# Gated DeltaNet and Hyena layer on one core: in levels two to five of the triangular inverse, VectorE's 32x32 block transposes in place of a ScalarE copy and TensorE transposes

## The reference

```python
kk = jnp.einsum('nbhid,nbhjd->nbhij', kc, kc)
a_strict = jnp.where(strict, bc[..., :, None] * kk * jnp.exp(diff), 0.0)
lower_unit = a_strict + jnp.eye(GDN_CHUNK, dtype=a_strict.dtype)
rhs = jnp.concatenate([vc * bc[..., None], kc * (bc * jnp.exp(gcum))[..., None]], axis=-1)
sol = lax.linalg.triangular_solve(lower_unit, rhs, left_side=True, lower=True, unit_diagonal=True)
```

## Time and profile before

| | us |
|---|---|
| runs | 1676.72, 1670.04, 1681.54; median 1676.72 |
| span of the profiled execution | 1665.2 |
| of it the heads and the tail | 162.8 to 775 |

### The profile page before, as it was taken

How to read it: one execution, slowest core, us unless ns; L and a number is a source line. 1 busy time by engine, 2 the same in 40 slices (tenths; PEclk the granted TensorE clock), 3 DMA queues, 4 the chain that set the end, 5 groups by cost and what they waited for, 6 DMA issues and landing times.

```text
span 1665.2 us, 26911 instructions
## 1 busy us (share of the span) xinstructions
PE 1611.4 (97%) x10066; PEld 1397.3 (84%) x10066; DVE 1151.5 (69%) x1701; ACT 766.9 (46%) x1281; POOL 116.2 (7%) x215
## 2 busy tenths in 40 slices
PE   5999999999999999999998999999999999999997
PEld 1247899899998999999998888888888888888886
DVE  3745889899998987776777655555555555655665
ACT  1345564555645556433346544444444444343331
POOL 1000110101101010000110000000000000111110
PEclk9999999999999999999999999999999999999999
DMA  9995353444534435223994345544554456877872
GB/s 370 390 387 223 121 184 129 144 163 142 172 121 165 152 129 197 103 86 126 356 334 171 126 179 200 202 175 179 200 202 177 178 200 229 288 245 253 281 247 100
DMA packets 83233, 334.06 MB, mean 201 GB/s; under 512 B 8059, under 2 KB 24502, under 8 KB 56706
## 3 DMA queue, kind: packets, MB, share of 16 engines
q1 hardware_dynamic: 62304, 257.97, 41.8%
q0 software_dynamic: 19600, 68.25, 12.2%
q10 hardware_dynamic: 1234, 6.57, 1.1%
HBM read 328.56 MB, written 4.19 MB: 200 GB/s over the span
## 4 chain that ended last, share of the span: by engine, by line
PE 83%; DMA 7%; DVE 6%; ACT 2%; issue 1%; DVEq 1%; POOL 0%; POOLq 0%; ACTq 0%
PE g L483 10%; PE o L483 10%; PE o L476 7%; PE o L477 7%; PE o L478 7%; PE g L484 5%; PE o L484 5%; DMA w_mod_tile_o<-in_w_mod_t 4%; PE g L559 2%; PE o L490 2%; PE g L490 2%; PE g L491 2%; PE g L492 2%; PE o L492 2%; PE o L491 2%; PE g L570 2%
## 5 line engine op out<-in xcount | busy, mean ns | idle before, releaser
L457 DVE TENSOR_TENSOR w_lo<-w_raw,w_hi 128x2048 fp32r<-128x2048 f32 x203 | 464.8, 2289 | 208.0 <-ACT w_hi L452 207.7
L452 ACT CAST w_hi<-w_raw 128x2048 fp32r<-128x2048 f32 x204 | 390.0, 1912 | 221.0 <-PE o L492 73.9
L476 PE MATMUL o<-h_hi,w_hi 128*128 128x256 f32 (+1 forms) x896 | 298.0, 333 | 3.2 <-DVE w_lo L457 1.8
L478 PE MATMUL o<-h_hi,w_lo 128*128 128x256 f32 (+1 forms) x896 | 282.1, 315 | 0.0
L477 PE MATMUL o<-h_lo,w_hi 128*128 128x256 f32 (+1 forms) x896 | 281.6, 314 | 0.0
L483 PE MATMUL g<-h_hi_lo,w_hi 128*128 128x512 f32 x704 | 245.0, 394 | 0.0
L483 PE MATMUL o<-h_hi_lo,w_hi 128*128 128x512 f32 x688 | 240.7, 394 | 0.6 <-DVE h_hi_lo L1961 0.6
L484 PE MATMUL g<-h_hi_lo,w_lo 128*128 128x256 f32 x704 | 195.0, 277 | 0.0
L484 PE MATMUL o<-h_hi_lo,w_lo 128*128 128x256 f32 x688 | 190.7, 277 | 0.0
L476 PEld LDWEIGHTS o<-h_hi,w_hi 128*128 128x128 f32 x896 | 171.4, 191 | 13.8 <-issue 6.4
L478 PEld LDWEIGHTS o<-h_hi,w_lo 128*128 128x128 f32 x896 | 170.7, 191 | 11.0
(11 more groups left out here) (383 smaller groups left out, 2789.4 us busy)
## 6 DMA issues: line engine op xcount, KB each, us to landing
w_raw<-in_w_ff_t SPq DMA_DIRECT2D x88, 1024.0 KB, 6.3
w_raw<-in_w_heads_t SPq DMA_DIRECT2D x56, 1024.0 KB, 4.9
w_mod_raw<-in_w_mod_t SPq DMA_DIRECT2D x32, 1024.0 KB, 10.6
w_raw<-in_w_down_t SPq DMA_DIRECT2D x32, 1024.0 KB, 7.0
w_mod_piece_h<-in_w_mod_t POOLq DMA_DIRECT2D x112, 256.0 KB, 3.5
w_raw<-in_w_out_t SPq DMA_DIRECT2D x16, 1024.0 KB, 8.0
w_mod_tile_o<-in_w_mod_t POOLq DMA_DIRECT2D x16, 1024.0 KB, 9.9
w_mod_piece_d<-in_w_mod_t POOLq DMA_DIRECT2D x64, 256.0 KB, 6.0
```

The source lines that it names most:

```text
L452: e.copy(whi[p.split[j]][:], raw[p.raw[j]][:]).then_inc(hi_ready, 1)
L457: e.tensor_tensor(wlo[p.split[j]][:], raw[p.raw[j]][:], whi[p.split[j]][:].bitcast(F32), ALU.subtract).then_inc(lo_ready, 1)
L476: e.matmul(o, a, xh, start=first, stop=False)
L478: return e.matmul(o, b, xh, start=False, stop=last)
```

## The change

At levels two to five the ScalarE copy `X{l}` and the four TensorE transposes `DN{l}` are left out. VectorE transposes `X` itself, straight from PSUM into `D`, with one instruction that transposes each 32x32 block in its place, drains, and multiplies `D` by the mask in SBUF. Level six keeps the old way. The tables of steps (`STEPS`), which give the semaphore counts, lose the steps. In the written orders `inv("D{l}")` moves up to directly behind `inv("DT{l}")`, ahead of the split `re(...)` that stood between them.

```diff
@@ inverse_pe @@
             elif step[:2] == "DN":
                 w_ia(pe, h, f"X{n}")
-                if n == 2:
-                    w_ia(pe, h, "qe")
                 for c in range(NCHUNK):
                     last = pe.transpose(Z[:, at_chunk(c)], bD[:, c], IDN)
@@ head_pe @@
-            inv("UT1"); scan("z3"); pr(15); scan("o3"); inv("DN2"); inv("Y2"); pr(16); inv("UT2"); pr(17); pr(18); pr(19)
+            inv("UT1"); scan("z3"); pr(15); scan("o3"); inv("Y2"); pr(16); inv("UT2"); pr(17); pr(18); pr(19)
@@ head_act @@
-                inv("X2"); scan("os"); ev(1); inv("Y2"); re(1); inv("X3"); inv("Y3"); re(2); th_(0); ev(2); inv("X4"); inv("Y4")
+                scan("os"); ev(1); inv("Y2"); re(1); inv("Y3"); re(2); th_(0); ev(2); inv("Y4")
@@ inverse_dve @@
+            elif step == "D6":
+                w_ip(v, h, "DN6")
+                last = v.tensor_tensor(bD[:], chunks(Z), mid(lev[:, 12]), mulv)
             elif step[0] == "D" and n > 1:
-                w_ip(v, h, f"DN{n}")
-                last = v.tensor_tensor(bD[:], chunks(Z), mid(lev[:, 6 + n]), mulv)
+                v.transpose(flat(bD), X[:, :])
+                v.drain()
+                last = v.tensor_tensor(bD[:], bD[:], mid(lev[:, 6 + n]), mulv)
@@ head_dve @@
-                cv(0); inv("M2"); inv("DT2"); re(0); inv("D2"); scan("nb"); inv("M3"); inv("DT3"); re(1); at_(); inv("D3")
-                inv("M4"); cv(1); inv("DT4"); re(2); cv(2); inv("D4"); sm(0); pc(12, 13); inv("M5"); inv("DT5"); re(3); pc(13, 14)
-                inv("D5"); sm(1); inv("M6"); pc(14, 15); inv("DT6"); pc(15, 16); cv(4); re(4); inv("D6"); sm(2); scan("mix")
+                cv(0); inv("M2"); inv("DT2"); inv("D2"); re(0); scan("nb"); inv("M3"); inv("DT3"); inv("D3"); re(1); at_()
+                inv("M4"); cv(1); inv("DT4"); inv("D4"); re(2); cv(2); sm(0); pc(12, 13); inv("M5"); inv("DT5"); inv("D5"); re(3)
+                pc(13, 14); sm(1); inv("M6"); pc(14, 15); inv("DT6"); pc(15, 16); cv(4); re(4); inv("D6"); sm(2); scan("mix")
```

More of the change, by code:

```diff
@@ L337, in build @@
         LV = range(1, 7)
-        STEPS = {"ip": ["tok", "dec", "dT", "kT", "qT", "kk", "u"] + [x for l in LV for x in (f"DN{l}", f"Y{l}", f"UT{l}") if x != "DN1"],
-                 "ia": ["lf0", "lf1", "vt", "sq", "e1", "e2", "qn", "kT", "qT", "qe"] + [x for l in LV for x in (f"X{l}", f"Y{l}") if x != "X1"],
-                 "iv": ["hv", "nr", "kt", "A", "U0", "D1", "ag"] + [x for l in LV for x in (f"M{l}", f"DT{l}", f"D{l}") if x != "D1"] + ["Z"],
+        STEPS = {"ip": ["tok", "dec", "dT", "kT", "qT", "kk", "u"] + [x for l in LV[:-1] for x in (f"Y{l}", f"UT{l}")] + ["DN6", "Y6", "UT6"],
+                 "ia": ["lf0", "lf1", "vt", "sq", "e1", "e2", "qn", "kT", "qT", "qe"] + [f"Y{l}" for l in LV[:-1]] + ["X6", "Y6"],
+                 "iv": ["hv", "nr", "kt", "A", "U0", "D1", "ag", "M1", "DT1"] + [x for l in LV[1:-1] for x in (f"M{l}", f"DT{l}", f"D{l}")]
+                        + ["M6", "DT6", "D6", "Z"],
                  "sp": ["z0", "s0", "k1", "z1", "s1", "k2", "z2", "s2", "k3", "z3"],
@@ L746, in head_pe @@
             scan("z2"); pr(10); scan("s2"); pr(11); scan("o2"); inv("u"); pr(12); scan("k3"); pr(13); inv("Y1"); pr(14)
-            inv("UT1"); scan("z3"); pr(15); scan("o3"); inv("DN2"); inv("Y2"); pr(16); inv("UT2"); pr(17); pr(18); pr(19)
-            inv("DN3"); inv("Y3"); pr(20); pr(21); inv("UT3"); pr(22); pr(23); inv("DN4"); inv("Y4"); pr(24); pr(25)
-            inv("UT4"); pr(26); pr(27); inv("DN5"); inv("Y5"); pr(28); inv("UT5"); pr(29); pr(30); inv("DN6"); inv("Y6")
+            inv("UT1"); scan("z3"); pr(15); scan("o3"); inv("Y2"); pr(16); inv("UT2"); pr(17); pr(18); pr(19)
+            inv("Y3"); pr(20); pr(21); inv("UT3"); pr(22); pr(23); inv("Y4"); pr(24); pr(25)
+            inv("UT4"); pr(26); pr(27); inv("Y5"); pr(28); inv("UT5"); pr(29); pr(30); inv("DN6"); inv("Y6")
             pr(31); scan("tr"); mod(); inv("UT6")
@@ L785, in tail_pe @@
             inv("kk"); scan("o2"); scan("z3"); pr(8); pr(9); inv("u"); scan("o3"); pr(10); inv("Y1"); pr(11); pr(12)
-            inv("UT1"); pr(13); inv("DN2"); inv("Y2"); scan("tr"); pr(14); inv("UT2"); pr(15); inv("DN3"); inv("Y3")
-            pr(16); inv("UT3"); pr(17); inv("DN4"); inv("Y4"); pr(18); inv("UT4"); pr(19); inv("DN5"); inv("Y5"); pr(20)
+            inv("UT1"); pr(13); inv("Y2"); scan("tr"); pr(14); inv("UT2"); pr(15); inv("Y3")
+            pr(16); inv("UT3"); pr(17); inv("Y4"); pr(18); inv("UT4"); pr(19); inv("Y5"); pr(20)
             inv("UT5"); pr(21); inv("DN6"); inv("Y6"); uh2(); pr(22); inv("UT6"); pr(23); hu(0); scan2("z0"); pr(24); scan2("s0"); hu(1)
@@ L1252, in head_act @@
                 inv("e2"); inv("qn"); ev(0); inv("kT"); uhc(); inv("qT"); inv("qe"); re(0); scan("vs2"); inv("Y1"); scan("vn3")
-                inv("X2"); scan("os"); ev(1); inv("Y2"); re(1); inv("X3"); inv("Y3"); re(2); th_(0); ev(2); inv("X4"); inv("Y4")
-                re(3); ev(3); th_(1); inv("X5"); inv("Y5"); ev(4); re(4); th_(2); inv("X6"); inv("Y6"); ev(5); tz()
+                scan("os"); ev(1); inv("Y2"); re(1); inv("Y3"); re(2); th_(0); ev(2); inv("Y4")
+                re(3); ev(3); th_(1); inv("Y5"); ev(4); re(4); th_(2); inv("X6"); inv("Y6"); ev(5); tz()
             def tail_act():
@@ L1308, in tail_act @@
                 scan("vs2"); inv("qn"); inv("kT"); inv("qT"); inv("qe"); ev(0); re(1); scan("vn3"); scan("os"); ev(1)
-                inv("Y1"); re(2); inv("X2"); inv("Y2"); ev(2); inv("X3"); inv("Y3"); re(3); inv("X4"); inv("Y4"); tz(); inv("X5"); ev(3)
+                inv("Y1"); re(2); inv("Y2"); ev(2); inv("Y3"); re(3); inv("Y4"); tz(); ev(3)
                 inv("Y5"); inv("X6"); re(4); inv("Y6")
```

## The result

The changed kernel takes 1693.09 us (median of 4 runs, 1692.24 to 1695.11) against 1673.38 us for the kernel before (median of 4, 1666.61 to 1681.54): ratio 1.0112, 95% interval 1.008 to 1.0145. It is slower by about 1%, though TensorE has 128 operations and ScalarE 32 copies less to do. A ratio with its interval is worked out from all runs of both kernels and is not the quotient of the two medians.

A forecast was written before the change was run, and what follows sets the result against it. VectorE and TensorE, balanced in the steady heads, were taken to bound the kernel. Six steady heads +14.4, head 0 +1.7 and tail -3.2 made +12.9 us on the 1676.7 us median: 1689.6, forecast as 1690, range 1680 to 1703.

The forecast's parts named there:

- VectorE is as full as TensorE: In steady heads VectorE has only 1 us of slack in 70.55, so the two engines are balanced.
- The removed work is worth nothing in the steady heads: ScalarE's 32 copies, 19 us, costed at nothing there; TensorE's 1.76 us a head less does not set the larger bound.
- The transpose, 0.68 us, 0.77 to the next start: Added VectorE block transpose at levels two to five: 0.68 us, 0.77 with drain, 3.08 us more a head.
- Rivals B: VectorE's transpose takes two passes over 32-bit data, 1.285 us: +16.9 us on top, 1706.5 us; chance 0.13.
- C: VectorE's transpose is cheaper than a pass, 0.487 us: -5.5 us, 1684 us; chance 0.09.
- D: Neither neighbour overlaps VectorE's transpose, another 0.16 us each: +4.5 us, 1694 us; chance 0.10.
- TensorE waits for w_lo some 1 us at four tile starts: In every steady head, splits end 1.37 us later against margins of 0.2 and 1.03 us, so TensorE waits.
- A steady head, +2.4 us: Each of six steady heads grows from 70.55 to about 73.0 us, +14.4 us in all.
- Bound (a): Steady head: VectorE never waits except for DMA, which gives 73.0 us.
- the ring (b): Steady head: loop from cv(5) through VectorE's split, TensorE's tile and ScalarE back to cv(5), giving 72.95 us.
- The tail, -3.2: After the steady heads, TensorE-bound; VectorE's waits have room for 3.08 us, so 4 x 0.44 + 1.4 is gained.
- The median stands 11.5 us above the span: Median of three runs, 1676.7 us, against the profiled span, 1665.2; the same shift was applied to the median.

The follow-up runs named there:

- Run 3: Kernel before, TensorE transposes and ScalarE copies kept, with an extra VectorE transpose and drain ahead of the mask multiply at levels two to five: 1693.61 us against 1676.98.
- Run 5: Kernel before with the changed way in levels two and three only, in all heads, VectorE's order as before: 1673.62 us against 1676.92.
- run 2: Changed kernel without the VectorE transpose and its drain, so its outputs are not the reference's: 1668.11 us against 1676.98 for the kernel before.
- run 1: Changed kernel with VectorE's steady-head list in the old order, D steps behind the splits again: 1684.34 us against 1676.98 for the kernel before.
- the second trace: Trace of the changed kernel run again, unaltered, beside the experiments: 1690.92 us against 1676.92 for the kernel before, ratio 1.0085.
- run 4: Kernel before with the changed way only in the last head, the tail: 1673.11 us against 1676.98, ratio 0.9982.
- laid out anew: Changed kernel with scalings and first state copy moved to ScalarE and VectorE's list reordered: 1723.98 us against 1676.92 for the kernel before.
- changed with masks on GpSimd: Changed kernel with each head's six products of A and mask moved from VectorE to GpSimd: 1697.99 us against 1677.82 for the kernel before.

## Why the prediction held, point by point

The forecast was 1690 us, slower by 0.8%; measured were 1693.09 and 1690.92 us, slower by 1.1% and 0.9%. The mechanism held in its steps; that the second median lies within 1 us of the forecast is partly luck, since two of its six runs are of the faster group (last section) and the sum was some 3 us too small.

- *VectorE is as full as TensorE.* Right. Run 3 shows it best: work put on VectorE alone costs 2.2 of 3.1 us a head. Run 5, half as much, costs 0.66, and in run 2 work taken off TensorE alone pays 0.7 of 1.76, there with the moved order.
- *The removed work is worth nothing in the steady heads.* Nearly: 1.6 us in seven heads (runs 1 and 3).
- *The transpose, 0.68 us, 0.77 to the next start.* 0.707 and 0.78. The estimate of 0.71 that the prediction gives beside its own figure was the nearer one. Rivals B (1.285 us) and C (0.487) are out by the duration. D is out too: the transpose starts 0.61 us after `DT`, and the split 0.61 after `D`'s product, so the neighbours overlap as without it.
- *TensorE waits for w_lo some 1 us at four tile starts.* 24 waits in six heads, 3.4 us a head.
- *A steady head, +2.4 us.* The term of the sum that was too small: from 228.65 to 654.62 before is 71.00 a head, from 230.07 to 673.06 after is 73.83, +2.83, and +2.62 in the second trace. VectorE's busy time was right: 387.0 us in six heads before, 403.5 after, 2.75 more in a head, where 3.08 less four gaps of 0.08 at drains was taken. What failed is the credit for its waits. Bound (a) let 3.8 us of them in six heads turn into work, so that with 24 new gaps its idle time should have gone from 38.9 to about 37.0 us; it went to 39.5 (38.3 in the second trace). The waits for `UT` and the transposes went, but of the 1.0 us for `hy_v` 0.8 stayed, and those for DMA, 2.1 us, became 3.5 (2.4 in the second trace).
- *Which bound holds.* I had taken the larger of two, VectorE's total (a) and the ring (b), and they came out alike. By (a) the order would not matter; run 1 shows that it does, by 0.75 us a head (73.83 and 73.08). In (b) it matters: with `D5` and its transpose behind the split the ring holds 0.60 + 0.77 = 1.37 less, 71.58 in place of 72.95, and has room. The waits fit that: in the changed kernel VectorE still waits for `hy_v`, where the ring closes, and in run 1 it never does. So the ring probably binds with the moved order and VectorE's total with the old one; this is argued from the waits, and no run changes the ring alone. With the old order (a) gives +2.45 and measured is +2.08; with the moved one both give +2.4 and measured is +2.83. A rule that takes the larger of two such bounds has missed by 0.4 us to either side; the idle time above says where the changed kernel lost it, and for the old order I have not shown why.
- *Head 0, +1.7.* 67.86 - 65.87 = +2.0, and +3.2 in the second trace.
- *The tail, -3.2.* -3.1, and run 4 has the same without the rest of the change.
- *The sum.* +12.9 forecast, +16.0 at the mixer's output, and +14 to +16 at the end, group against group (last section).
- *The median stands 11.5 us above the span.* I took this as it stood. In the other traces the time of the profiled run is 1.6 to 3.4 us above its span (1695.11 against 1693.4 in the changed kernel); the rest is there because the profiled run, by its 2310 matmuls, was of the faster of two groups of runs.

## What to carry to other kernels

Before work is moved from the busiest engine to a less busy one, look at the stretch where it lies and count the idle time of the receiver that is a wait, not a gap at a drain: here 1 us a head, and everything above it was paid. On an engine that is full, the order of its list is a price too: an instruction put ahead of the one that others wait for makes them late, here by 0.75 us a head, for four transposes with their products. Relief bought nothing here where it fell in the other half of the loop, or on an engine that shares a path with the one relieved; that it would count ahead of the late instruction is what I would try next, and no run shows it.

## What the runs showed of the hardware

**GpSimd and VectorE take turns on SBUF by whole instructions.** A 128x512 fp32 product takes 1.16 to 1.19 us on GpSimd where nothing is in its way (0.686 on VectorE), 2.21 us where a w_lo subtraction runs, and VectorE's next instruction waits for it: 0.426 became 1.21 us, and two elements took 1.14. I had expected a slower pace at most. The Trainium skill (SBUF — State Buffer, Who interferes with whom) says that VectorE and GpSimd share a pair of ports under an exclusive lock, that a VectorE instruction with two SBUF inputs contends with a GpSimd one that reads SBUF, and that one with at most one SBUF input and in no two-port mode does not. The trace agrees for `w_lo`, `attn` and `k_silu` (0.749 us became 0.947 on average), and for `DT` on the other side (0.685 us in both). The two-element instruction has one SBUF input and was held up too; in which mode it ran the trace does not tell.

**TensorE's matmul stretch has two paces at one granted clock.** From 1000 to 1400 us, behind all edits, the traces show 2309 or 2310 matmuls in four kernels (before; two levels; laid out anew; changed with masks on GpSimd) and 2265 to 2267 in the ten others, all at a granted clock of 1.00. The time of the profiled run goes with the count: each of the four lies in the lower part of its kernel's runs (of the kernel before the span alone tells, 1665.2 us). The times fall apart likewise: of 73 runs of the kernel before, 20 lie between 1665.9 and 1671.6 us and 53 between 1675.0 and 1682.3, none between, the means 1668.8 and 1678.3. The changed kernel had 1692.2 to 1695.1 in its first four runs, and later 1684.7 and 1685.2 beside 1690.8 to 1693.4. Group against group the change is worth some 16 us and 14 to 15 us. In the heads the paces can't be seen: 71.00 us a head in the trace of before, 70.94 in that with the tail alone changed, at the other pace. That the pace makes the groups is the likeliest reading: the stretch of matmuls above takes 9.1 us longer at the slower pace, and the group means lie 9.5 us apart. What sets it no run shows. It can put a ratio of two medians of a few runs wrong by half a per cent.

**The block transpose.** 32x32 blocks, 128x512 fp32 from PSUM: 0.707 us (0.703 to 0.710 in 32), against 0.693 for the product of the same shape behind it; a drain behind it makes 0.78.
